# Attention values joined over two cycles, the mask of the maxima moved to VectorE, and the output weights split during heads 1 to 5

## The reference

```
s = einsum('bqhd,bkhd->bhqk', q, k) * HEAD_DIM**-0.5     # 2048 frames, 8 heads
s = s + c[q] - c[k]                                      # c: running sum of log forget gates
p = softmax(where(k_pos <= q_pos, s, -inf))
fox_out = (p @ v) * silu(g_fox)
mem_out = softmax(mq @ mk^T) @ mv * silu(g_mem)          # 4 heads, 256 tokens, no mask
out = x + concat([fox_out, ssm_out, mem_out]) @ w_out    # w_out is 1024 x 1024
```

## Time and profile before

| what | value |
|---|---|
| median of 3 runs | 1434.78 us (1432.9 to 1437.66) |
| the profiled execution's own time | 1428.78 us |
| its span, first to last instruction | 1427.1 us |
| PE busy | 1383.0 us (97%) |
| DVE busy | 926.3 us (65%) |
| ACT busy | 635.2 us (45%) |
| POOL busy | 559.8 us (39%) |
| DMA moved | 275.82 MB, mean 193 GB/s |
| mean granted TensorE clock | 0.996 of full |

### The profile page before, as it was taken

The page is one execution under the profiler, slowest core; times in us unless marked ns, Lnnn a source line. Parts: engine busy times, 40 slices in busy tenths (PEclk is TensorE's granted clock), DMA queues, the critical chain, the costliest instruction groups (busy, mean ns, idle before and its releaser), DMA issues.

```text
span 1427.1 us, 25010 instructions
## 1 busy us (share of the span) xinstructions
PE 1383.0 (97%) x8510; PEld 1101.7 (77%) x8510; DVE 926.3 (65%) x1772; ACT 635.2 (45%) x1364; POOL 559.8 (39%) x587
## 2 busy tenths in 40 slices
PE   8999989999999999999999999999999999799998
PEld 8999767788877767777777777777777777578886
DVE  4789755692466787665333766676676666697784
ACT  6766423432443364445332555555554556432221
POOL 1121432200033243212000566676775659544442
PEclk9999999999999999999999999999999999899999
DMA  7885699987369679678996945725726514346552
GB/s 230 304 285 189 221 250 243 321 260 211 91 162 326 206 224 301 220 251 261 333 294 187 247 126 113 156 56 116 156 57 130 125 33 126 98 152 217 181 186 86
DMA packets 207565, 275.82 MB, mean 193 GB/s; under 512 B 49424, under 2 KB 146096, under 8 KB 203952
## 3 DMA queue, kind: packets, MB, share of 16 engines
q1 hardware_dynamic: 206400, 274.22, 65.8%
q10 hardware_dynamic: 1040, 0.00, 0.0%
HBM read 186.93 MB, written 86.00 MB: 191 GB/s over the span
## 4 chain that ended last, share of the span: by engine, by line
PE 59%; DVE 5%; issue 2%; POOL 2%; ACT 2%; DMA 1%; SPq 1%; DVEq 0%; ACTq 0%; POOLq 0%
PE in_g L927 13%; PE attn_pv L2518 11%; PE attn_s L2487 6%; PE attn_s L2586 6%; PE attn_s L2492 5%; PE attn_s L2470 5%; PE attn_pv L2586 4%; PE attn_s L2500 2%; PE in_b L1102 1%; POOL in_hv L1810 1%; PE in_b L1054 1%; PE attn_s L2489 1%; PE attn_s L2473 1%; PE attn_s L2541 1%; PE in_b L1157 1%
## 5 line engine op out<-in xcount | busy, mean ns | idle before, releaser
L927 PE MATMUL in_g<-in_wh,in_xh 128*128 128x512 f32 (+2 forms) x904 | 331.3, 380 | 4.9 <-DVE in_wl L1521 1.9
L927 PE MATMUL in_g<-in_wl,in_xh 128*128 128x512 f32 (+2 forms) x904 | 321.7, 369 | 0.0
L2828 DVE TENSOR_REDUCE attn_tops<-attn_s 128x1 f32<-128x512 f32 (+3 forms) x288 | 159.7, 617 | 126.6 <-PE attn_s L2470 110.3
L927 PE MATMUL in_g<-in_wh,in_xl 128*128 128x512 f32 (+2 forms) x904 | 234.6, 378 | 1.4 <-DVE in_xl L1532 1.3
L2790 POOL TENSOR_TENSOR attn_probs<-attn_probs,attn_probs_turned 128x512 f32<-128x512 f32 (+3 forms) x190 | 202.1, 1064 | 86.1 <-ACT attn_probs_turned L2618 64.1
L2618 ACT ACTIVATE attn_probs_turned<-attn_s 128x512 f32<-128x512 f32 (+1 forms) x352 | 161.4, 545 | 144.9 <-PE attn_s L2492 144.6
L927 PEld LDWEIGHTS in_g<-in_wh,in_xh 128*128 128x128 f32 x904 | 165.5, 189 | 39.7 <-issue 6.2
L927 PEld LDWEIGHTS in_g<-in_wl,in_xh 128*128 128x128 f32 x904 | 165.5, 189 | 28.0
L927 PEld LDWEIGHTS in_g<-in_wh,in_xl 128*128 128x128 f32 x904 | 157.8, 189 | 34.4 <-issue 5.2
L1808 POOL TENSOR_SCALAR in_hs<-in_hs 128x8 f32<-128x8 f32 (+1 forms) x53 | 21.3, 402 | 398.6 <-DVE in_hs L1559 398.6
L2518 PE MATMUL attn_pv<-attn_probs_turned,attn_v 128*64 128x256 f32 (+1 forms) x1216 | 144.8, 368 | 0.1
(11 more groups left out here) (379 smaller groups left out, 2716.3 us busy)
## 6 DMA issues: line engine op xcount, KB each, us to landing
in_xu<-scratch_xt SPq DMA_DIRECT2D x87, 512.0 KB, 5.5
in_xl<-scratch_xt SPq DMA_DIRECT2D x34, 512.0 KB, 4.6
in_raw<-in_w_in SPq DMA_DIRECT2D x40, 256.0 KB, 5.3
scratch_xt<-in_xu SPq DMA_DIRECT2D x19, 512.0 KB, 4.6
scratch_xt<-in_xl SPq DMA_DIRECT2D x17, 512.0 KB, 4.5
scratch_k<-in_x_turned SPq DMA_DIRECT2D x17, 512.0 KB, 7.0
scratch_q<-in_x_turned SPq DMA_DIRECT2D x17, 512.0 KB, 5.3
in_x_turned<-in_x_prompt SPq DMA_DIRECT2D x16, 512.0 KB, 4.7
```

What stands on the lines that cost most here:

```text
L927: last = X.matmul(g_ps[b][:, 0:m], x, ws[:, c, w0:w0 + m], start=(c == 0 and h == 0 and ws is wh), stop=(c == KC - 1 and h == 1))
L2828: V.tensor_reduce(top_parts[:, joined[u.n] % 2, i, k // 4:k // 4 + 1], bank[:, 0:n, :].rearrange("p n k -> p (n k)"), AX.X, ALU.max).then_ ...
```

## The change

- `TOGETHER` = 2: the values of two cycles are issued together, at the end of each odd cycle (the last two cycles stay single), so 45 groups of values instead of 88. Dens are placed in odd cycles only.
- The mask of the maxima: PE's matmul L2473 goes. VectorE reduces the whole tiles as before, and takes the diagonal tile by itself with one `tensor_tensor_reduce`, which adds the mask and reduces. All fox units now go through `top_parts` and end in two last reductions.
- The first maxima come two thirds of a visit earlier, and the lead is 24 instead of 20.
- `w_split` and `w_low` move from head 7 to 16 places in heads 1 to 5 (`W_AT`), by halves of a chunk. The queries' buffers aren't free there, so ACT writes the high half to one staging buffer, `w_stage`, POOL takes the low half from it, and SP stores it to DRAM (`w_hi`, `store_w`), behind that head's loads and stores; in head 7 SP loads all 4 MB back. ACT's next `w_split` waits for POOL and for the store.
- `t_split` and `t_low_early` come earlier in head 7, and `late` goes: POOL adds most blocks of head 7's last unit too.

```diff
@@ -369,9 +369,9 @@
     for n in range(7):
         beside[gate + 2 + n, 1] = [("early_in", n)]
 
-    for n in range(HOOKS - 1):
-        beside[NV - 1, n + 1] = [("attention", n)]
-    order = projection_order(items, visits, behind, beside) + [("attention", HOOKS - 1)]
+    for n, at in enumerate(((NV - 2, 2), (NV - 1, 0), (NV - 1, 1))):
+        beside[at] = [("attention", n)]
+    order = projection_order(items, visits, behind, beside)
 
     def upto(v, passes, each=1):
 
@@ -1881,11 +1881,15 @@
 
 TILES_EACH = 4
 UNITS = (("fox", 0), ("fox", 4), ("mem", 0), ("mem", 4), ("fox", 8), ("fox", 12))
-CYCLE, TOGETHER = 4, 1
+CYCLE, TOGETHER = 4, 2
 
 HOOKS = 3
 EARLY = 4
-LEAD = (6, 6, 5, 5, 5, 5)
+LEAD = (6, 6, 6, 6, 6, 6)
+
+
+W_CHUNKS = (0, 4, 1, 5, 2, 6, 3, 7)
+W_AT = (17, 20, 23, 26, 29, 32, 35, 38, 41, 44, 47, 50, 53, 56, 59, 62)
 
 
 def attention_units():
@@ -1902,8 +1906,7 @@
         where = {(u.n, k): b for b, (u, k, _) in enumerate(scores)}
         halves = 0
         for u in units:
-            late = u.head == FOX_HEADS - 1 and u.blocks > 12
-            mine = [k for k, _ in u.scores if u.kind == "fox" and (late or u.blocks > 8 and k in (2, 3, 6, 10))]
+            mine = [k for k, _ in u.scores if u.blocks > 8 and k in (2, 3, 6, 10)]
             for engine, ks in (("pool", [k for k, _ in u.scores if k not in mine]), ("vector", mine)):
                 pair = len(ks) > 1 and dict(u.scores)[ks[1]] == 0
                 for i, k in enumerate(ks):
@@ -1962,15 +1965,15 @@
         if 1 <= scores[CYCLE * c][0].head <= KC // 2 and scores[CYCLE * c][:2] == (units[len(UNITS) * scores[CYCLE * c][0].head + 4], 8):
             order.append(("t_sums", scores[CYCLE * c][0].head - 1))
         n = c - first
-        if 1 <= n <= KC:
-            order += [("w_split", n - 1, 0), ("w_split", n - 1, 1), ("w_low", n - 1)]
-        if n in (KC, KC + 1):
-            order += [("t_split", n - KC), ("t_low_early", n - KC)]
+        if c in W_AT:
+            order += [(what, W_AT.index(c)) for what in ("w_split", "w_low", "w_out")]
+        if n in (1, 3):
+            order += [("t_split", n // 2), ("t_low_early", n // 2)]
         if n == HALF:
             order.append(("gated", 0))
     assert rows == len(units) and upto == len(tops) and not ended[cycles - 2]
-    order += [("product", 0, 0), ("product", 0, 1)] + [("den", n) for n in ended[cycles - 1]]
-    order += [("first_sum", 0), ("t_split", 2), ("t_split", 3), ("mix", 1)]
+    order += [("both", n) for n in ended[cycles - 1]] + [("product", 0, 0), ("first_sum", 0), ("product", 0, 1)]
+    order += [("den", n) for n in ended[cycles - 1]] + [("t_split", 2), ("t_split", 3), ("mix", 1)]
 
     order += [("fold", 1), ("halves", 1, "A11"), ("t_low", 2), ("t_low", 3), ("product", 0, 2), ("y", 0, 0), ("mix", 2)]
     order += [("fold", 2), ("raw", 1, 0), ("raw", 1, 1), ("halves", 1, "S2"), ("product", 0, 3), ("y", 0, 1)]
@@ -2063,7 +2066,7 @@
     sums = Sums(units, scores)
     SCORES, ALL = len(scores), len(units)
 
-    joined = [sum(1 for u in units[:n + 1] if u.kind == "fox" and u.first) for n in range(ALL)]
+    joined = [sum(1 for u in units[:n + 1] if u.kind == "fox") for n in range(ALL)]
 
     def head_end(head):
 
@@ -2102,7 +2105,7 @@
             identr, causr = (over.sb(k, [P, P], F32R) for k in ("identr", "causr"))
             negmax = over.sb("negmax", [P, 2, P], F32R)
         probs = a.sb("probs", [P, 2, 4, 4, P])
-        top_parts = a.sb("tops", [P, 2, EACH, 4])
+        top_parts = a.sb("tops", [P, 2, EACH, 5])
         den = a.sb("den", [P, 2, EACH])
 
         rfox, rmem = a.sb("rfox", [P, PROMPT_TILES, FOX_HEADS]), a.sb("rmem", [P, PROMPT_TILES, MEM_HEADS])
...
@@ -2313,6 +2316,11 @@
                 sp.wait_ge(s_lo, halves_upto(q - 1, name))
             sp.dma_start(raw[name][:, 0:SSM // P, :], D.ssm[:, t * P:(t + 1) * P].rearrange("(c p) t -> p c t", p=P))\
                 .then_inc(s_ssm[i], 16)
+
+        def store_w(sp, n):
+            cols = slice(n % 2 * 512, (n % 2 + 1) * 512)
+            sp.wait_ge(s_wh, n + 1)
+            sp.dma_start(D.w_hi[W_CHUNKS[n // 2]][:, cols], w_stage).then_inc(s_w_out, 16)
 
         def load_x(sp, q):
             if q == 0:
@@ -2377,12 +2385,19 @@
                 load_queries_keys(sp, head)
                 load_values(sp, head)
                 store(sp, head - 2)
+                for x in order:
+                    if x[0] == "w_out" and head - 1 == W_AT[x[1]] // (head_end(0) // CYCLE):
+                        store_w(sp, x[1])
                 if head - 2 < HALF:
 
                     sp.wait_ge(s_t, 4 * (head - 1))
                     for k in range(2):
                         sp.dma_start(D.t34[k, head - 2], stage[:, k, :]).then_inc(s_t_out, 16)
             store(sp, FOX_HEADS - 2)
+            sp.wait_ge(s_score, head_end(FOX_HEADS - 2))
+            sp.wait_ge(s_w_out, 16 * 2 * KC)
+            for c in range(KC):
+                sp.dma_start(fl(w_hi[c]), D.w_hi[c]).then_inc(s_w[c % HALF], 16)
             load_x(sp, 0)
             store_tail(sp, 0)
             load_mix(sp, 0)
@@ -2466,16 +2481,13 @@
                             last = X.matmul(bank[:, at:at + n, :], mqb[h][0:LANE, q], mkb[h][0:LANE, keys],
                                             start=True, stop=True)
                         else:
-                            masked = k + n == u.first + i + 1
                             last = X.matmul(bank[:, at:at + n, :], qb[h][0:LANE, q], kb[h][0:LANE, keys],
-                                            start=True, stop=not masked)
-                            if masked:
-                                last = X.matmul(bank[:, at + n - 1, :], identr[:, :], causr[:, :], start=False, stop=True)
+                                            start=True, stop=True)
                     last.then_inc(s_mx, 1)
                 if what == "row":
                     u = units[s]
-                    if u.kind == "fox" and u.first:
-                        pe.wait_ge(s_neg, joined[s])
+                    if u.kind == "fox":
+                        pe.wait_ge(s_neg, 2 * joined[s])
                     else:
                         pe.wait_ge(s_top, top_end[s + 1])
                     X.matmul(bank[:, 0, :], negmax[:, s % 2, :], identr[:, :], start=True, stop=True).then_inc(s_row, 1)
@@ -2545,7 +2557,9 @@
                     at, left, weights = (PAIR if q else ONE)[j]
                     pe.wait_ge(s_lo, halves_upto(q, left))
                     if q == 0 and j == 0:
-                        pe.wait_ge(s_wl, KC)
+                        pe.wait_ge(s_wl, 2 * KC)
+                        for c in range(HALF):
+                            pe.wait_ge(s_w[c], 16 * 4)
 
                         pe.wait_ge(s_exp, SCORES)
                     if q == 0 and j == 1:
@@ -2629,11 +2643,13 @@
                     F(out[:, h, at:at + EACH // 2, :], v_ps[s % 2][:, 0:EACH // 2, :], ACT.Copy).then_inc(s_copy, 1)
                 if what == "w_split":
 
-                    act.wait_ge(s_t, 4 * (s % HALF + 1))
-
-                    act.wait_ge(s_score, head_end(FOX_HEADS - 2))
-                    cols = slice(rest[0] * 512, (rest[0] + 1) * 512)
-                    F(w_hi[s][:, cols], w_raw[:, s, cols], ACT.Copy).then_inc(s_wh, 1)
+                    c, cols = W_CHUNKS[s // 2], slice(s % 2 * 512, (s % 2 + 1) * 512)
+                    act.wait_ge(s_t, 4 * (c % HALF + 1))
+                    if s:
+
+                        act.wait_ge(s_wl, s)
+                        act.wait_ge(s_w_out, 16 * s)
+                    F(w_stage.bitcast(F32R), w_raw[:, c, cols], ACT.Copy).then_inc(s_wh, 1)
                 if what == "t_split":
                     i = s
                     act.wait_ge(s_t, 4 * HALF)
@@ -2738,9 +2754,9 @@
                     pool.wait_ge(s_t, 4 * c + 3)
                     G.tensor_tensor(stage[:, 1, :], b21, t2_raw[:, c, :], ALU.subtract).then_inc(s_t, 1)
                 if what == "w_low":
-                    c = s
-                    pool.wait_ge(s_wh, 2 * (c + 1))
-                    G.tensor_tensor(w_lo[:, c, :], w_raw[:, c, :], fl(w_hi[c]), ALU.subtract).then_inc(s_wl, 1)
+                    c, cols = W_CHUNKS[s // 2], slice(s % 2 * 512, (s % 2 + 1) * 512)
+                    pool.wait_ge(s_wh, s + 1)
+                    G.tensor_tensor(w_lo[:, c, cols], w_raw[:, c, cols], w_stage, ALU.subtract).then_inc(s_wl, 1)
                 if what == "t_low_early":
                     i = s
                     pool.wait_ge(s_th, i + 1)
@@ -2811,26 +2827,33 @@
                     u, parts = tops[s]
                     i, k, n, _ = parts[0]
                     bank = ring_ps[ring.at[what, s]]
-                    alone, last = u.kind == "mem" or u.first == 0, s + 1 == top_end[u.n + 1]
+                    last, d = s + 1 == top_end[u.n + 1], joined[u.n] % 2
                     dve.wait_ge(s_mx, s + 1)
-                    if (alone or last) and u.n >= 2:
```

(26 more changed lines are left out.)

5 lines of the change are left out of this document (3 added, 2 removed).

## The result

The changed kernel took 1443.64 us (median of 11 runs, 1437.90 to 1452.76). Against the kernel before the ratio is 1.0072, with an interval from 1.0057 to 1.0086: some 9 us slower where the prediction said 21 faster. The profiled execution took 1451.76 us (span 1449.7, granted clock 0.982), one of the slowest of the eleven.

A forecast was written before the change was run, and what follows sets the result against it. PE's own pace was taken to bound heads 0 to 6, something else head 7. Terms -12 - 15 - 12 - 1 + 5 + 14 = -21 gave 1407.8, plus 6.0 to the median: 1414 us, range 1397 to 1434.

The forecast's parts named there:

- Masks, -12: Taking 128 mask matmuls off PE at the maxima saves 12 us, between 10.9 and 15.7.
- Head 7, -12: Moving `w_low` and the VectorE adds out of head 7 removes two PE stalls and half clock: 12 us, bounds 6 to 13.
- Start, -1: At the start of attention, earlier hooks shorten the maxima's wait for VectorE: 0 to 2 us, taken as 1.
- VectorE's price: Each diagonal TTR takes 0.45 us, adding 5.3 us a head on VectorE, still not the bound on average.
- Staging, +14 (3 to 28): Weight copies in heads 1 to 5 stall ACT, then PE: 9.8 us, plus 4 of half clock behind two long stalls.
- Joining, -15, with +5 for bursts: 43 fewer groups of values on PE save 15 us; PE waiting for late VectorE maxima costs 5, bounds 0 and 25.
- 0.35 for each change to values and back: PE's price per switch between scores and values: 0.14, 0.10 and 0.11 us together, 15 us for 43.
- the two borders, 0.10 and 0.11: On PE, 0.10 us extra in the starts after a values group, 0.11 from `row` to the first values.
- the cover: 1.87 us of values between one cycle's maxima and the next scores, gone in even cycles; PE loses 0.5 to 0.7 a head.
- The rival "joining gives nothing": The change of shape is paid within a values group too, so joining saves nothing: 1429 us, chance 0.08.
- The rival "late stores": `store_w` lands in 8.1 us, not 2.3, in four places behind loads, adding 23 and 6 of half clock: 1443, chance 0.10.
- The rival of VectorE as the bound: A TTR over 1.04 us makes VectorE the bound; at 1.24 a head takes 56 us: about 1436, chance 0.12.

The follow-up runs named there:

- free places: Whole change with the sixteen output-weight copies moved to cycles clear of a head's loads and GpSimd's sums, against the kernel before: 1424.11 us, ratio 0.9920.
- the weights alone: Kernel before with only the output weights' move and the last unit's adds back on GpSimd, at the change's own places: 1438.98 us, ratio 1.0031.

## Why the prediction was wrong

The runs can be strung from before to after, each link one edit, the first two: 1435.0, mask and weights at free places -23.7 (1411.3), lead and first maxima -2.1 (1409.2), joining +14.9 (1424.1), the change's own places +19.5 (1443.6). Set against the prediction's terms:

- **Masks, -12.** Right: -11.5 (9.8 by the ratio), and 0.097 us each between the two rows of 0.085 and 0.12.
- **Head 7, -12.** Right: -11.6 in the weights alone at free places, from 62.3 to 50.9 us. Both stalls and the half clock behind them went, as forecast.
- **Start, -1.** At most the -2.1 that it shares with the lead; too small for these runs.
- **VectorE's price.** Right: 0.43 for the TTR, and VectorE is not the bound, though its late `both` holds PE in joined cycles. With GpSimd busy for most of each head the TTR's first instruction took 282 to 300 ns in all 128 cases: that agrees with the Trainium skill (SBUF — State Buffer, section Who interferes with whom), by which it should not be held up.
- **Staging, +14 (3 to 28).** The places were right, four behind a head's loads and cycle 17 behind GpSimd's sums; cycle 29, behind the second sums, was missed, but cost PE nearly nothing. Alone it cost 15.5, with joined cycles 19.5. PE's stalls were sized well in sum: 9.8 forecast, 9.9 in the weights alone (three waits, 5.07 the longest), and in the whole change 10.5 in cycles 17, 26, 38, 47 and 59 (2.27, 1.60, 1.69, 3.40, 1.54, for 2.9, 1.2, 0.5, 4.2, 1.0). What was too small is the half clock, put at 4 and behind the two long stalls only. In the weights alone it was 12 x 0.28 + 14 x 0.24 = 6.7 (clock 0.72 from 888 to 900 and 0.76 from 1046 to 1060). In the profiled execution of the whole change, 8 us above its median, it was 20.2 over heads 1 to 5 by the rows above, and came behind stalls of 1.5 to 1.7 too.
- **Joining, -15, with +5 for bursts.** This is the step that failed: 10 forecast as a gain, 14.9 measured as a loss. Of the two halves, "0.35 for each change to values and back" was too large. The 0.14 inside a group is there (0.15 measured), but the two borders, 0.10 and 0.11, mostly do not go: `row` still stands ahead of the values and a `den` behind or ahead of them, and these borders are changes of shape too. The net was 0.13 a pair, some 6 us over the whole, not 15. At free places even these 6 us hardly show, since waits and clock alone make up 13.9 of the 14.9. The other half, the cover, was named but at the wrong place. The prediction looked at VectorE's maxima and the banks; there the waits were small (the largest for maxima, 1.2 us, stands ahead of a den too). PE waited instead for `both` ahead of the den (5.2 us), for exps and for the row's copy. In single cycles 1.9 us of values stand between one cycle's work and the next; behind an even cycle of a pair nothing does. The den shows that the missing cover is the main cause: moved behind the values it gave 10.9 joined, and took the waits for `both` away. In single cycles it gave nothing by the ratio and 0.5 a head, some 4 us, by the traces, so 7 to 11 of the 10.9 belong to the cover.

So, in this order of edits, the miss of some 30 us is 25 from joining and 5.5 from staging. It is also an interaction, which the prediction's sum of terms has no place for: joining costs 1.0 on the kernel before and 14.9 on the one with mask, lead and weights, and the weights' places cost 4 us more in joined cycles. That joining has used up ACT's slack is a likely reason for the 4, not a shown one. The rival "joining gives nothing" (0.08, 1429) described this nearest, and was itself too mild. The rival "late stores" gave 1443, near the measured number, but only by luck: it needed landings over 6 us, and the 16 stores landed in 2.0 to 5.5. Its 8.1 us was a misreading besides: the view in the earlier trace rows holds two loads of `scratch_t` with its eight stores; the stores by themselves (L2384) landed in 2.0 to 2.4, the loads in 5.7 to 8.1. The rival of VectorE as the bound is refuted by its busy time and by the 0.43, where it needed 1.04.

Three things stay open. Why joining costs so much more once the mask and the lead are changed was not taken apart. Why joined cycles cost more in head 0 was not separated from the clock, which differed at its start from run to run. And the pairs that stand the other way round in every second head were only shown to be slower, not followed wait by wait.

The best kernels found are the whole change at free places with single cycles, 1409.2 (ratio 0.9819), and the same with the den behind the values (0.9823): 1.8% faster than before.
